# A two-layer diffusion backbone: the output projection, the norm and the first up units as one ordered stream, and a down stage entered without a barrier

## The reference

```python
def ada_params(cvec, w, b):
    return jnp.split(jax.nn.silu(cvec) @ w + b, 6, axis=-1)
def pre_mod(x, g, shift, scale):
    return rms_norm(x, g) * (1 + scale) + shift
def post_add(x, y, g, gate):
    return x + gate * rms_norm(y, g)
def conv_ffn(h, w_up, conv_w, conv_b, w_down):
    u = h @ w_up                                   # 2 x 2688 channels
    up = jnp.pad(u, ((0, 0), (1, 1), (0, 0)))
    u = up[:, :-2] * conv_w[0] + up[:, 1:-1] * conv_w[1] + up[:, 2:] * conv_w[2] + conv_b
    a, b = jnp.split(u, 2, axis=-1)
    return (jax.nn.gelu(a) * b) @ w_down
...
        x = post_add(x, y, mix_post_g[l], g1)      # y = mixer output @ w_out
        f = conv_ffn(pre_mod(x, ffn_pre_g[l], sh2, sc2), ffn_w_up[l], ...)
        x = post_add(x, f, ffn_post_g[l], g2)
```

## Time and profile before

| | before |
|---|---|
| median of 3 runs | 1632.71 us (1629.73 to 1634.76) |
| the profiled execution | 1634.82 us |
| its span | 1633.0 us |
| TensorE products busy | 1513.7 us, 93% of the span |
| VectorE, ScalarE, GpSimd busy | 968.6, 728.8, 598.6 us |
| chain that ended last | TensorE 83%, VectorE 7%, ScalarE 3% |
| mean granted clock of TensorE | 0.974 of full speed |

### The profile page before, as it was taken

The page is one execution under the profiler, slowest core; times in us unless marked ns, Lnnn a source line. Parts: engine busy times, 40 slices in busy tenths (PEclk is TensorE's granted clock), DMA queues, the critical chain, the costliest instruction groups (busy, mean ns, idle before and its releaser), DMA issues.

```text
span 1633.0 us, 22238 instructions
## 1 busy us (share of the span) xinstructions
PE 1513.7 (93%) x7560; PEld 1213.0 (74%) x7560; DVE 968.6 (59%) x1465; ACT 728.8 (45%) x1240; POOL 598.6 (37%) x529
## 2 busy tenths in 40 slices
PE   6889798989999999998999788899997999999997
PEld 1777466768888888886888576677776788887886
DVE  2458588548678666833334575788874544444455
ACT  3332476534323333323353445487773544443453
POOL 1352254242222222221333531365542444443454
PEclk9999799999999999999999999899999999999999
DMA  9120750104355334411221111110001333332222
GB/s 340 41 88 10 244 196 27 52 30 125 117 168 162 116 121 141 129 39 40 64 67 59 58 53 58 59 40 1 1 1 52 91 103 90 103 90 65 87 93 103
DMA packets 129135, 143.85 MB, mean 88 GB/s; under 512 B 7160, under 2 KB 95484, under 8 KB 129064
## 3 DMA queue, kind: packets, MB, share of 16 engines
q1 hardware_dynamic: 129064, 142.91, 27.7%
HBM read 140.79 MB, written 2.10 MB: 87 GB/s over the span
## 4 chain that ended last, share of the span: by engine, by line
PE 83%; DVE 7%; ACT 3%; DMA 2%; POOL 2%; issue 2%; SPq 0%; POOLq 0%; DVEq 0%; ACTq 0%
PE ps L462 23%; PE ps L463 22%; PE ps L464 22%; PE ps L1400 4%; PE ps L1386 3%; PE ps L1411 2%; PE ps L1413 2%; DVE hT_lo L781 1%; DVE hT_hi L779 1%; DMA start_w<-in_ada_w_dram 1%; DMA ada_w<-in_ada_w_dram 1%; PE ps L1303 1%; PE ps L666 1%; PE ps L1839 1%; POOL w_lo L454 1%
## 5 line engine op out<-in xcount | busy, mean ns | idle before, releaser
L454 POOL TENSOR_TENSOR w_lo<-raw,w_hi 128x1024 fp32r<-128x1024 f32 (+1 forms) x184 | 348.3, 1894 | 644.8 <-ACT w_hi L447 644.7
L462 PE MATMUL ps<-hT_hi,w_hi 128*128 128x512 f32 (+1 forms) x1072 | 383.7, 358 | 6.7 <-DVE hT_lo L781 5.8
L463 PE MATMUL ps<-hT_lo,w_hi 128*128 128x512 f32 (+1 forms) x1072 | 381.2, 356 | 0.0
L464 PE MATMUL ps<-hT_hi,w_lo 128*128 128x512 f32 (+1 forms) x1072 | 378.8, 353 | 0.0
L447 ACT ACTIVATE w_hi<-raw 128x1024 fp32r<-128x1024 f32 (+1 forms) x200 | 172.8, 866 | 191.3 <-PE ps L464 166.8
L462 PEld LDWEIGHTS ps<-hT_hi,w_hi 128*128 128x128 f32 x1072 | 202.8, 189 | 46.1 <-DVE hT_lo L781 10.0
L464 PEld LDWEIGHTS ps<-hT_hi,w_lo 128*128 128x128 f32 x1072 | 202.0, 188 | 30.0
L463 PEld LDWEIGHTS ps<-hT_lo,w_hi 128*128 128x128 f32 x1072 | 202.8, 189 | 27.8
L2062 DVE TENSOR_TENSOR g_lo<-act_g,g_hi 128x768 fp32r<-128x768 f32 (+1 forms) x84 | 106.7, 1277 | 164.6 <-ACT g_hi L2012 163.3
L462 PE MATMUL ps<-w_hi,g_hi 128*128 128x512 f32 x420 | 166.6, 397 | 3.5 <-DVE g_lo L2062 3.0
L463 PE MATMUL ps<-w_lo,g_hi 128*128 128x512 f32 x420 | 164.0, 391 | 0.0
(11 more groups left out here) (234 smaller groups left out, 2533.4 us busy)
## 6 DMA issues: line engine op xcount, KB each, us to landing
raw<-in_ffn_w_up_dram SPq DMA_DIRECT2D x84, 512.0 KB, 3.9
ada_w_up<-in_ada_w_dram SPq DMA_DIRECT2D x48, 512.0 KB, 4.1
raw<-in_ffn_w_down_dram SPq DMA_DIRECT2D x84, 256.0 KB, 2.6
ada_w<-in_ada_w_dram SPq DMA_DIRECT2D x32, 512.0 KB, 4.9
start_w<-in_ada_w_dram SPq DMA_DIRECT2D x8, 1024.0 KB, 10.7
raw<-in_c_w_qkv_dram SPq DMA_DIRECT2D x12, 512.0 KB, 3.6
raw<-in_ab_w_in_dram SPq DMA_DIRECT2D x8, 512.0 KB, 4.4
raw<-in_ab_w_out_dram SPq DMA_DIRECT2D x8, 512.0 KB, 3.5
```

The lines of the kernel that those rows point to most:

```text
L454: by.tensor_tensor(w_lo[:, slot, 0:width], raw[:, n % RAW, 0:width], w_hi[:, slot, 0:width].bitcast(F32), ALU.subtract).then_inc(lo_split, 1)
L462: nc.tensor.matmul(outp, s_hi, m_hi, start=first, stop=False, skip_group_check=True)
L463: nc.tensor.matmul(outp, s_hi, m_lo, start=False, stop=False, skip_group_check=True)
L464: return nc.tensor.matmul(outp, s_lo, m_hi, start=False, stop=last, skip_group_check=True)
```

## The change

The barriers ahead of the FFN norm, of the up stage and of the down stage are taken out, in both layers, and with them the phases' closings (a layer now closes 5 phases and not 7). In place of the norm stage:

- The transposes of the FFN norm go in steps (`norm_steps`) through banks 6, 7 and 5. Layer 0: 8 steps of one chunk over the four latent tiles, then 4 steps of two chunks over the two context tiles. Layer 1: 4 steps of two chunks over tiles 0 and 1, then 4 over tiles 2 and 3. The first three steps stand inside the last batch of the output projection, which is now (1,4) with (1,5), or (1,2) with (1,3).
- `up_first_tensor` makes units 0, 1 and 2 together: for each step of the first group three units' products and a transpose step further ahead, then the second group unit by unit.
- ScalarE, VectorE and GpSimd get orders in which the late tiles' post-norm stands between the steps. In layer 1 the gate products move into the first batch, behind its second chunk, and VectorE splits the low part of unit 2.
- The first down unit's activation is split within the last up turn, into the unused fourth slot of `w_hi` and `w_lo`; each tile pair of that unit waits for the taps that free its banks.
- In layer 0 the multiply-adds of layer 1's conditioning stand behind units 2 to 5 of a turn, the loads behind weight units 4, 5 and then 0, 1 of the next turn, and the summing products ahead of unit 2.

```diff
         def out_batches(l, nt):
             if l == 1:
-                return [[(1, 0), (1, 1)], [(0, 3)], [(1, 2)], [(1, 3)]]
-            return [[(0, t)] for t in range(OUT_DONE[l], nt)] + [[(1, t)] for t in range(nt)]
+                return [[(1, 0), (1, 1)], [(0, 3)], [(1, 2), (1, 3)]]
+            return [[(0, 4)], [(0, 5)], [(1, 0)], [(1, 1)], [(1, 2)], [(1, 3)], [(1, 4), (1, 5)]]
+        TURN_BANKS = (6, 7, 5)
+        TURN_BEHIND = ({6: (0,), 7: (1, 2)}, {3: (0,), 4: (1,), 5: (2,)})
+        MID_TILES = (((0, 1, 2, 3), (4, 5)), ((0, 1), (2, 3)))
...
+        def norm_steps(l):
+            if l == 0:
+                return ([((0, 1, 2, 3), 0, k, 1) for k in range(KC)] + [((4, 5), 1, k, 2) for k in range(0, KC, 2)])
+            return [(tiles, 0, k, 2) for tiles in ((0, 1), (2, 3)) for k in range(0, KC, 2)]
...
+        def mid_turn(pe, l, j):
+            tiles, _, k0, nk = norm_steps(l)[j]
+            tag, w = f"ffn{l}", len(tiles) * P
+            pe.wait_ge(s("norm_xn"), norm_base(tag, "xn") + tiles[-1] + 1)
+            if j >= 3:
+                pe.wait_ge(s("norm_split"), norm_base(tag, "split") + 2 * (j - 2))
+            for i in range(nk):
+                k = k0 + i
+                for n, t in enumerate(tiles):
+                    mm = nc.tensor.transpose(bank(TURN_BANKS[j % 3])[:, i * w + n * P:i * w + (n + 1) * P],
+                                             xn[:, t, k * P:(k + 1) * P], ident[:, :])
+            mm.then_inc(s("norm_turned"), 1)
...
+        def up_first_tensor(pe, l):
...
+            for j in range(first):
+                mid_wait_split(pe, l, j)
+                for i in range(steps[j][3]):
+                    for u in range(3):
+                        if j == 0 and i == 0:
+                            wait_split(pe, phase, u)
+                        product(u, j, i)
+                    if l == 1 and j == first - 1 and i == 0:
+                        mid_turn(pe, l, first)
+                if l == 0 or j + 3 < first:
+                    mid_turn(pe, l, j + 3)
+            if l == 1:
+                for j in range(first + 1, first + 3):
+                    mid_turn(pe, l, j)
+            for u in range(3):
+                for j in range(first, len(steps)):
+                    if u == 0:
+                        mid_wait_split(pe, l, j)
+                    for i in range(steps[j][3]):
+                        mm = product(u, j, i)
+                    if u == 0 and j == first:
+                        mid_turn(pe, l, first + 3)
+                mm.then_inc(used[phase], 1)
...
         def out_scalar(act, l, nt):
+            if l == 0:
...
+                up_split(0)
+                x_square(act, "ffn0", tag, nt, 3)
+                up_split(1)
+                mid_shift(act, l, 0)
+                up_split(2)
+                mid_shift(act, l, 1)
+                mid_shift(act, l, 2)
+                second_half(4)
+                second_half(5)
+                mid_shift(act, l, 3)
+                x_square(act, "ffn0", tag, nt, 4)
+                mid_shift(act, l, 4)
+                x_square(act, "ffn0", tag, nt, 5)
+                for j in range(5, len(norm_steps(l))):
+                    mid_shift(act, l, j)
...
         def out_vector(dve, l, nt):
+            if l == 0:
...
+                for j in range(3):
+                    mid_split(dve, l, j)
+                gated(4)
+                mid_split(dve, l, 3)
+                added(4)
+                gated(5)
+                mid_split(dve, l, 4)
+                added(5)
+                mid_split(dve, l, 5)
+                x_normed(dve, then, 4)
+                mid_split(dve, l, 6)
+                x_normed(dve, then, 5)
+                for j in range(7, len(norm_steps(l))):
+                    mid_split(dve, l, j)
+            else:
...
+                mid_split(dve, l, 0)
+                mid_split(dve, l, 1)
+                dve.wait_ge(lo_split, FIRST_UNIT[f"up{l}"] + 2)
+                split_lo(dve, f"up{l}", 2, 1024, by=nc.vector)
+                mid_split(dve, l, 2)
+                gated(2)
+                gated(3)
+                added(2)
+                added(3)
+                mid_split(dve, l, 3)
+                x_normed(dve, then, 2)
+                x_normed(dve, then, 3)
...
         def up_sync(sp, l):
+            def turn(i, ada_ends, ada_begins):
...
+                    if ada_begins and m >= MAC_AT + 2:
+                        if m == MAC_AT + 2:
+                            sp.wait_ge(s("mixpost0_post"), post_count(ALL_T, ALL_T - 1, 1))
+                        ada_pair(i, m - (MAC_AT + 2))
+                    if ada_ends and m < MAC_AT:
+                        ada_pair(i - 1, m + KC // 2 - MAC_AT)
...
         def down_tensor(pe, l, nt):
-            after_phase(pe, before)
             gate_tensor(pe, l, tag, 1, (0, 1))
...
+                    if first and not half:
+                        pe.wait_ge(s(f"taps{l}"), TURNS * TURN + t // 2 + 1)
```

More of the change, by code:

```diff
@@ new lines, in post_gate, with post_add @@
+        def post_gate(dve, tag, nt, t, acc, y1):
+            dve.wait_ge(s(f"{tag}_ysq"), square_at(tag, nt, 1, t) + 1)
+            if t >= 2:
+                dve.wait_ge(s(f"{tag}_post"), post_count(nt, t - 2, 3, tag))
+            nc.vector.tensor_tensor(y1, acc, gate[:, int(t >= LAT_T), BANK:D], ALU.mult).then_inc(s(f"{tag}_post"), 1)
+        def post_add(dve, tag, nt, t, y0, y1):
+            dve.wait_ge(s(f"{tag}_yr"), 3 * t + 3)
+            dve.wait_ge(s(f"{tag}_post"), post_count(nt, t, 1, tag))
+            for half, y in enumerate((y0, four(y1))):
+                xv = four(x[:, t, half * BANK:(half + 1) * BANK])
+                nc.vector.scalar_tensor_tensor(out=xv, in0=y, scalar=rms[:, t:t + 1], in1=xv,
+                                               op0=ALU.mult, op1=ALU.add).then_inc(s(f"{tag}_post"), 1)
@@ L1715, in out_tensor @@
                             mm.then_inc(s(f"{tag}_acc"), 1)
[L1716 to L1725 removed]
+                    if last and k in (1, 3, 5):
+                        mm.then_inc(s(f"out{l}_w_used"), 1)
@@ new lines, in out_pool @@
+        def out_pool(pool, l, nt):
+            tag, then = f"mixpost{l}", f"ffn{l}"
+            early, late = MID_TILES[l]
+            for t in early:
+                post_root(pool, tag, nt, t)
+                if t:
+                    x_rms(pool, then, t - 1)
+            x_rms(pool, then, early[-1])
+            split_lo(pool, f"up{l}", 0, 1024)
+            split_lo(pool, f"up{l}", 1, 1024)
+            if l == 0:
+                split_lo(pool, f"up{l}", 2, 1024)
+            for t in late:
+                post_root(pool, tag, nt, t)
+            for t in late:
+                x_rms(pool, then, t)
@@ L1873, in turn @@
                         split_hi(act, f"down{l}", m - (TURN - 3), BANK, free=False)
+                    if last and m == 3:
+                        down_activation(act, l, nt, 0, 0, first=True)
                     if not b:
@@ L1940, in up_vector @@
                 turn(i, l == 0)
-            turn(TURNS - 1, False)
+            turn(TURNS - 1, False, last=True)
             close(dve, "dve")
```

446 lines of the change are left out of this document (255 added, 191 removed).

## The result

| | before | after |
|---|---|---|
| median | 1632.01 us (4 runs, 1629.73 to 1634.76) | 1606.52 us (4 runs, 1604.79 to 1611.55) |
| ratio after to before | | 0.9848 (0.9821 to 0.9875) |
| the profiled execution, its span | 1634.82, 1633.0 us | 1606.59, 1604.8 us |
| TensorE products busy | 1513.7 us, 93% | 1503.7 us, 94% |
| mean granted clock | 0.974 | 0.982 |

The kernel is 25.5 us faster, at 1606.5 where 1605.5 was forecast.

A forecast was written before the change was run, and what follows sets the result against it. TensorE was taken as the bound, standing still or slow in two middles and two passages. Gains of 8.9 + 8.3 + 6.0 + 5.0 = 28.2 us from the median 1632.7, plus 1.0 for a clock dip, gave 1605.5 us; range 1600.5 to 1612.5.

The forecast's parts named there:

- Middle of layer 0: Last output products, norm and first three up units of layer 0: 55.2 us falls to 46.3, gain 8.9 us.
- step 5: Sixth transpose step of layer 0's middle: TensorE stalls 2.3 us, as ScalarE's square of tile 5 queues ahead of shift 5.
- restarts: TensorE's slower start after each stop: 0.1 us for each of some seven in layer 0, 0.6 us in layer 1.
- The spare of tile 3: Layer 0's last latent tile is normed at about 7.7 us, first transposes come at 9.5: hidden with 1.8 us to spare.
- Middle of layer 1: From batch (0,3) to the third up unit's end in layer 1: 49.2 us falls to 40.9, gain 8.3 us.
- Passages: Up stage to down stage, barrier removed: gain 6.0 us in layer 0 and 5.0 us in layer 1.
- Conditioning steps: Layer 1's parameter multiply-adds, loads and summing products moved later in the up stage: left at zero, no waits there.
- The clock term: 1.0 us added for one clock dip at an even chance in each layer's middle; a dip loses 1.6 us.
- The sum: Gains of both middles and both passages: 28.2 us, giving 1604.5 us from the median and a forecast of 1605.5.
- Only the passages pay: Rival: the middles lose all they win through stalls; 11 us of gain remain, 1621.5 us; chance 0.05.
- Feeders slower: Rival: VectorE and GpSimd steps stretch beside each other in the middles, 1612 us; with several dips 1609 to 1614, chance 0.22.
- Slower: Rival: an early stall in the middles keeps the clock at 0.5 until three units end, 1651 us; chance 0.01.

The follow-up runs named there:

- e8_square_late: The kernel after with ScalarE's square of tile 5 put behind its shift 5 in layer 0; 1604.29 us, ratio 0.9839 to before.
- e7_split_behind: The kernel after with GpSimd's first weight split held until VectorE has scaled tile 3 (layer 0) or tile 1 (layer 1); 1605.22 us, one execution.
- e9_before_third: The kernel before, unchanged, run for a third trace; 1629.8 us.
- e4_steps_moved: The kernel before with only layer 1's conditioning steps moved, loads and sums included; 1633.54 us, ratio 1.0008 to before.
- e2_passages: The kernel before with only the entry to the down stage changed (no barrier, first activation split early); 1623.61 us, ratio 0.9942 to before.
- e6_late_norm: The kernel after with the scaling of the last latent tile done three times in layer 0; 1610.17 us, one execution.
- e3_middles: The kernel after with the barrier ahead of the down stage put back in both layers; 1619.88 us, ratio 0.9926 to before.

## Why the prediction was right

**Middle of layer 0.** Forecast 46.3 us from the end of (1,3) to the third up unit, measured 46.0 (340.7 to 386.74); gain forecast 8.9, measured 8.8, or 7.3 against the two other kernels with an unchanged middle. Stops, as gaps between products less the usual distance (0.35 for each four transposes between them): step 0 0.4 (forecast 0.4), unit 2's low part 0.5 (0.55), step 5 1.65 (2.3), tile 5's scaling 0.5 (0.7), steps 10 and 11 1.3 (1.5). The sum is 4.3 instead of 5.5. What was too small is the estimate for restarts: 1.6 us in place of 0.7, since the first product behind each block of transposes is followed after 0.31 to 0.34 us and not 0.23, with or without a stop. The two errors nearly cancel. e8_square_late shows the cause of the largest one.

**The spare of tile 3** was mis-sized: 0.7 us and not 1.8. The scaling ended 8.9 us after the end of (1,3) instead of 7.7, because beside GpSimd's splits it took 2.88 us. In e7_split_behind, where it took 0.75, it ended after 6.7: the rest of the chain was priced 1.0 us too long, the scaling 2.1 too short. The row it was priced by the earlier trace rows had no split beside it.

**Middle of layer 1.** Forecast 40.9 us, measured 39.9; gain 9.2 to 9.4 against 8.3. The stop of 1.5 us before the transposes of tiles 2 and 3 did not appear: they started at 1252.58 without a wait. The first split behind them cost 0.9 (forecast 1.0), the three shorter ones 1.3 (1.4), and the restarts 1.3 (0.6).

**Passages.** Layer 0 6.0 us, as forecast; layer 1 5.0, as forecast, between the first two profiles. But with the same instructions the old layer 1 passage took 6.9 us in three traces and 8.5 in two, so 3.4 is as good a number. The difference is the clock behind the barrier: its mean is 0.64 from 1505.8 to 1510.6 in before, 1.00 from 1502.4 to 1505.8 in e9_before_third. The forecast was made from one execution and could not see that 1.6 of its 5.0 us were a dip that comes and goes.

**Conditioning steps** at nothing: borne out by e4_steps_moved within 0.2% in whole time, and by an up stage without a wait. But its trace has the 3.1 us longer projection of layer 1, and 46 packets on q8 where before and e2_passages have 43, so a loss in that place that comes with these steps is not ruled out.

**The clock term** of 1.0 us was for dips in the two streams. By its own terms, 1.6 us at an even chance in each of two, it should have been 1.6. There were none (1.00 in both); e6_late_norm shows that a stop of 2.9 us in that place brings one, at 1.7 us, the size read from the earlier trace rows.

**The sum.** Over three traces each, before's mean span is 1630.0 and after's 1604.5 us, 25.5 apart. The changed stretches give 8.8, 6.1, 9.3 and 3.9 (the last because of the shorter passage in two traces of before), 28.1. The projection of layer 1 gives back 4.8 (113.8 to 118.6), and the other stretches together win 2. So the forecast's 28.2 of gain held for the places changed, its 1605.5 lies 1.0 under the median, and a loss of some 5 us in a place that the change does not touch was not in it. The places and mechanisms were forecast; that the total came within 1.0 us is in part luck, for the 4.8 us lost in the projection were nearly made up by 2.2 won elsewhere, by the dips that did not come (1.0) and by a before whose median turned out 0.7 lower.

**The rivals.** "Only the passages pay" falls with e3_middles. "Feeders slower" (whose four terms add up to 8.2 us, not 7) had its mechanism right in part: one instruction took nearly four times as long beside GpSimd, held up by it rather than stretched, but it had time to spare; the stream as a whole was no longer. The Trainium skill's page "GPSIMD Engine Reference", specifications table, has VectorE collide with GpSimd either with two SBUF inputs or in a perf mode that uses two ports. The scalings have one SBUF tensor in and did collide, 2.88 against 0.75 us; that fits the second case, but no run here shows the mode. "Slower" needed a clock that stays at 0.50; one dip followed a forced stop and no more.

## What to carry to other kernels

Lay the queues of all engines beside one another, instruction by instruction with durations from the trace: where an instruction that waits for something late stands ahead of one that others need (ScalarE's square ahead of a shift), the stall can be read off before it is built, and moving the instruction took 1.9 us out of it. Price an instruction of VectorE by a row in which GpSimd does what it will be doing, not by the cleanest row: here it ended only behind the GpSimd instruction begun before it. And before a gain is judged by the end of the profile, cut both traces at the same products, several executions of each: a stretch that no edit touches moved by 2 to 7 us here, up to more than a quarter of what the change was worth.

## What the runs showed of the hardware

- VectorE's scaling of a tile (128x1024, one SBUF tensor in, one out) took 0.75 us alone and 2.88 beside GpSimd's splits; it ended 0.55 us behind the end of the split begun before it, three times out of three. GpSimd's pair of splits took 5.20 us beside it and 4.74 alone.
- A stop of TensorE of 0.9 to 2.1 us sometimes brings a dip of the granted clock to 0.50 for up to 4 us (1.7 us lost) and sometimes does not, in the same kernel at the same instruction: in the three traces of after the pair of stops of 0.89 us had one behind it in two, the stop of 1.83 in one, that of 2.05 in two.
- Behind a block of transposes the first product is followed after 0.31 to 0.34 us instead of 0.23, at the full clock.
- A 512 KB weight load beside a packet of the instruction queue kept ScalarE waiting 3.8 to 5.3 us, without one 3.3 to 3.8. Why is open.
